# Bias table, its store and the last gate rows earlier in the second FFN of a two-block kernel

## The chip, the cores and the metric

The program runs on one core of one Trainium2 chip. The metric is the device time of that core in microseconds (us), less is better. A core has TensorE (PE, the matrix engine, with PEld for its weight loads), VectorE (DVE), ScalarE (ACT), GpSimd (POOL) and SyncE (SP). SP issues nearly all transfers (DMA) from one queue, in program order, and the core's 16 DMA engines carry them out.

## The reference

Two transformer blocks in sequence work on 256 tokens of width 1024. The first has a SwiGLU feed-forward network (FFN), a mixer of attention and convolution, and a second FFN. The second block has two attentions, an MLP and a gated embedding. All is in float32. The part in which the change lies is the end of the first block:

```python
def swiglu(h, w13, w2):
    gu = jnp.einsum('bsd,df->bsf', h, w13)
    g, u = jnp.split(gu, 2, axis=-1)
    return jnp.einsum('bsf,fd->bsd', jax.nn.silu(g) * u, w2)
...
        mod = (jnp.einsum('bd,dn->bn', c_act, w_ada[l]) + b_ada[l]).reshape(b, N_SUB, 3, D_MODEL)
...
        h = modulate(x, norm_w[l, 2], mod[:, 2, 0], mod[:, 2, 1])
        x = x + 0.5 * mod[:, 2, 2][:, None, :] * swiglu(h, ffn_w13[l, 1], ffn_w2[l, 1])
```

`D_FF` is 2816, that is 22 column blocks of 128. The gate `mod[:, 2, 2]` has 1024 columns, or eight blocks of 128 (numbers 64 to 71 of the 72 in `mod`). The second block of the network needs two tables: cosines and sines of the axial rotary embedding times the norm's gains, and for its dilated attention a bias by relative position (`bias_table[bucket]`, with the band's mask), which is the same for every query but shifted.

## The kernel before

**Weights come in units.** All weights lie in one array in the order of use, cut into units of 128 partitions x 2048 columns (1 MB). Every unit is loaded by SP into one of four raw buffers (`sb_raw`, NR = 4). ACT then writes its rounded half ("hi", `sb_ring`), in two halves of 1024 columns; DVE writes the remainder ("lo", L200), also in two halves. The ring of split units has four places (NS = 4). A matrix product takes three matmuls for each tile: hi x hi, lo x hi, hi x lo. A unit of the FFN's up projection holds the 16 tiles of one column block j, so PE uses one unit for each j, with moving tiles of 258 columns (256 tokens and 2 for the shift).

**A unit of gate rows** (`ada`) is loaded in the same way and in the same four raw buffers, but goes to no matmul: DVE multiplies its two row blocks with silu(c) and sums them (L209, two instructions of 128x1024 and two short reads). The list `ADA_3` says ahead of which unit of the second FFN each of its four gate units stands: position p is ahead of the weights of column block p.

**The order of the work** is written by a planner (`Plan`) as one list of steps; each engine runs those of the list that are its own, in that order. A raw buffer is refilled when its unit has been consumed: the load of unit i on SP waits for the "lo" (or the gate rows) of unit i-4, and SP's later transfers wait behind it. While PE works on block j+1, the planner has ACT and DVE finish block j (`glu_evac2`, below "the finish of block j") and split the weights of block j+3: on ACT the order is hi of j+3, the two shifts of block j (`sb_zb`), silu, `hid_hi`; on DVE two scalings from the banks, first half of lo of j+3, the product, second half of lo, `hid_lo`. The banks form a ring of seven; two are used for each block.

**The tables.** `load_tables` (SP, five small transfers of 960 KB in all, into `R`), `axial_tables` (DVE, seven instructions: one on `sb_bhalf` and six on `R`, which wait for the transfers), `bias_table` (one PE matmul in full float32, 128x512, then one addition on DVE into 12 partitions of `R`) and `bias_store` (SP: the 12 rows of 512 numbers are written to `scratch` in main memory 64 times each, 768 pieces of 2 KB, 1536 KB). `bias_store` waits for the addition. The second block reads the rows back, each with its own shift (`load_bias`), some 200 us later.

In the kernel before, `load_tables` and `axial_tables` stand behind the finish of block 4, `bias_table` and `bias_store` behind that of block 8, and the last gate unit is ahead of block 17.

Of the kernel before, what the change touches and what calls it, by code (L numbers as in the profile page):

```python
# [36 lines left out]
def unit_list():  # L37
# [5 lines left out]
    def chunks(tiles, n=16):  # L43
        return [("w", tiles[i:i + n]) for i in range(0, len(tiles), n)]

    def down(m, n, k0=0):
        return [tile(m, k0 + k, f) for f, ks in down_order(n) for k in ks]
# [4 lines left out]
    def ada_pairs(first, n):  # L52
        return [ada(first + i, first + i + 1) for i in range(0, n, 2)]

    def mix(ws, adas, places):
        out = []
        assert len(adas) == len(places)
        for i, w in enumerate(ws):
            out += [a for a, p in zip(adas, places) if p == i]
            out.append(w)  # L60
        return out

    def ffn_up(m, js):
        return [("w", [t for k in range(8) for t in (tile(m, k, j), tile(m, k, 22 + j))]) for j in js]

    def nat(m, ranges):
        w = sum(b - a for a, b in ranges)
        ks = U // w
        return [("w", [(m, k, a, b) for k in range(k0, k0 + ks) for a, b in ranges]) for k0 in range(0, 8, ks)]
# [22 lines left out]
    ws = ffn_up("w13b", range(22)) + chunks(down("w2b", 22))  # L92
    out += mix(ws, ada_pairs(64, 8), ADA_3)
    ws = nat("win2", [(1024, 1536)]) + nat("win2", [(0, 512)]) + nat("win2", [(512, 1024)])
# [19 lines left out]

ADA_1 = [1, 3, 4, 5, 8, 10, 11, 13, 13, 15, 17, 17, 19, 19, 21, 23]
ADA_2 = [0, 4, 4, 4, 13, 14, 15, 19]
ADA_3 = [5, 6, 9, 17]

PACE, AHEAD, KEEP = 4, 3, 2
TAKE_AFTER = (1, 2, 3)  # L120
# [130 lines left out]
def done(turn, *events):  # L251

    turn.buf.free = events
# [235 lines left out]
class Plan:  # L489
# [546 lines left out]
    def second_ffn(self):  # L1036
        m = self.m
        bk = Ring(m.banks[0:7])
        norm = []

        def begin(k):
            if k == 4:
                norm.append(self.x_norm("f2"))

        def finish(k):
            if k == 2:
                self.norm_rows(norm[0])

        first = self.glu2("f2", bk, 0, begin)
        for j in range(1, NH1):  # L1050
            banks = self.glu2("f2", bk, j, finish if j == 1 else None)
            if j == 1:
                self.glu_evac2("f2", first, 0)
            self.glu_evac2("f2", banks, j)
            if j == 4:
                self.add("load_tables")
                self.add("axial_tables")
            if j == 8:
                b = m.banks[7].take()
                self.add("bias_table", b)  # L1060
                done(b, ("bias_table",))
                self.add("bias_store")
        self.add("gcol", 2, 0.5)
        for f, bank in self.down("f2", bk, NH1, "down"):
            self.residual("f2", f, bank, "m2", True)
# [2419 lines left out]
```

How the kernel before makes its waits and increments, by code:

```python
    def then_inc(self, signal, n):  # L177
        if self.ins is not None:
# [11 lines left out]
    def wait_ge(self, signal, value):  # L190
        if self.passed.get(signal.name, 0) < value:
            self.passed[signal.name] = value
            if self.e is not None:
                self.e.wait_ge(signal.sem, value)
# [287 lines left out]
    def turn(self, *turns):  # L482
        for t in turns:
            for event in t.before:
                self.e.wait_ge(*self.at(*event))
# [930 lines left out]
    def load(self, i):  # L1417
        m, e = self.m, self.e
        if i >= NR:
            kind, blocks = m.units[i - NR]
            if kind == "ada":
                e.wait_ge(*self.at("ada", blocks[-1][1]))
            else:
                e.wait_ge(*self.at("lo", m.windex[i - NR], 1))
        w = m.widths[i]
        src = m.wts[m.offs[i]:m.offs[i] + 128 * w].rearrange("(p w) -> p w", p=128)
        e.dma_start(m.raw[:, i % NR, 0:w], src).then_inc(*self.up(f"unit{i % NR}_in", ("unit", i), by=16))
# [7 lines left out]
    def load_mask(self):  # L1435
        m, e = self.m, self.e
        e.wait_ge(*self.at("x", "f1", 7))
        e.dma_start(m.reg(34, 256), m.cons2_in[:, 0:256]).then_inc(*self.up("mask_in", ("mask",), by=16))
# [1 line left out]
    def load_tables(self):  # L1440
        m, e = self.m, self.e
        e.wait_ge(*self.at("merged_lo", 7))
        e.dma_start(m.reg(45, 256), m.cons2_in[:, OK2["axc"][0]:OK2["axc"][1]]).then_inc(
            *self.up("cosines_in", ("cosines",), by=16))
        e.dma_start(m.reg(44, 256), m.cons2_in[:, OK2["axs"][0]:OK2["axs"][1]]).then_inc(
```

## Time and profile before

| | |
|---|---|
| time, median of 3 runs | 1005.85 us (1005.77 to 1007.15) |
| the profiled execution | 1007.17 us, of which its span is 1005.4 us |
| PE busy | 988.8 us (98%) |
| DVE busy | 771.0 us (77%) |
| ACT busy | 536.6 us (53%) |
| DMA engines, queue of SP | 59.6% of 16 engines, 213 GB/s in the mean |

The times of the rows below are microseconds from the start of the span. A row of the timeline gives start, duration, engine, line, operation, what it writes and reads, and in square brackets how long the engine was idle before it and what ended that. The second FFN's up projection (22 blocks) runs from about 384 to 506 us. Matmul ends are modelled, so a row of PE can seem to overlap the next.

### The profile page before, as it was taken

Reading aid. Unit: us, or ns where it says so; the run is one execution under the profiler, and the core shown is the slowest. Engines: PE = TensorE matmul, PEld = TensorE weight load, DVE = VectorE, ACT = ScalarE, POOL = GpSimd, SP = SyncE. Lnnn points to the kernel's source line nnn. Section 1 sums busy time; section 2 is a strip of 40 time slices with the busy share of each in tenths; the row PEclk is TensorE's granted clock in tenths of the full one; section 3 lists DMA queues with packets and bytes.
Section 4 is the critical chain, followed back from the end, with each engine's and each line's share of the span. In section 5 each row is a group of like instructions: output and inputs, shape, how many; then the busy total and the mean of one; then the engine's idle time right before and its main releaser. Section 6 shows DMA issues by size and latency. Waiting matters only on the chain.

```text
span 1005.4 us, 17440 instructions
## 1 busy us (share of the span) xinstructions
PE 988.8 (98%) x7090; PEld 925.3 (92%) x7090; DVE 771.0 (77%) x1397; ACT 536.6 (53%) x930; POOL 12.0 (1%) x33
## 2 busy tenths in 40 slices
PE   8999999999899999999999999999999999999997
PEld 8999998998898999999988988789999988988896
DVE  6999999879976788685776688547778776677665
ACT  5555554437575565353665446664555554455453
POOL 0000000004000000000000000000000000000000
PEclk9999999999999999999999999999999999999999
DMA  8997998865563555677665435364445555545431
GB/s 334 372 352 260 372 345 327 314 200 211 220 224 130 206 211 184 234 216 230 244 215 201 170 126 209 126 196 126 161 168 181 186 190 187 202 176 177 179 106 42
DMA packets 33678, 213.94 MB, mean 213 GB/s; under 512 B 3773, under 2 KB 6717, under 8 KB 8894
## 3 DMA queue, kind: packets, MB, share of 16 engines
q1 hardware_dynamic: 33310, 211.78, 59.6%
q8 instruction: 56, 0.92, 0.4%
q10 hardware_dynamic: 288, 1.05, 0.3%
q14 instruction: 24, 0.20, 0.1%
HBM read 210.19 MB, written 2.62 MB: 212 GB/s over the span
## 4 chain that ended last, share of the span: by engine, by line
PE 81%; DVE 8%; ACT 4%; DMA 4%; issue 2%; SPq 0%; ACTq 0%; DVEq 0%
PE bank L224 79%; DMA sb_raw<-wts 3%; DVE sb_ring L200 2%; ACT sb_ring L197 2%; PE bank L227 2%; ACT sb_tmp L197 1%; DVE sb_tq L200 1%; DVE sb_junk L209 1%; DVE sb_tmp L200 1%; DMA sb_x<-xt 1%; DMA R<-rows 1%; DVE sb_tmp L206 1%; ACT R L197 0%; DVE R L200 0%; DVE R_512r L200 0%
## 5 line engine op out<-in xcount | busy, mean ns | idle before, releaser
L224 PE MATMUL bank<-sb_h,sb_ring 128*128 128x258 f32 (+2 forms) x3776 | 493.7, 291 | 0.6 <-ACT sb_h L197 0.3
L224 PEld LDWEIGHTS bank<-sb_h,sb_ring 128*128 128x128 f32 x3776 | 472.8, 189 | 14.5 <-issue 2.4
L200 DVE TENSOR_TENSOR sb_ring<-sb_raw,sb_ring 128x1024 fp32r<-128x1024 f32 (+1 forms) x324 | 386.3, 1206 | 10.4 <-ACT sb_ring L197 10.3
L197 ACT ACTIVATE sb_ring<-sb_raw 128x1024 fp32r<-128x1024 f32 (+1 forms) x324 | 320.4, 1037 | 72.0 <-DMA sb_raw<-wts 37.5
L224 PE MATMUL bank<-R_512r,sb_ring 128*128 128x256 f32 (+1 forms) x1608 | 225.7, 301 | 0.0
L224 PEld LDWEIGHTS bank<-R_512r,sb_ring 128*128 128x128 f32 x1608 | 211.5, 188 | 12.0 <-issue 0.5
L224 PE MATMUL bank<-sb_ring,sb_h 128*128 128x512 f32 (+1 forms) x504 | 112.5, 378 | 0.0
L224 PEld LDWEIGHTS bank<-sb_ring,sb_h 128*128 128x128 f32 x504 | 87.4, 188 | 16.6
L209 DVE CUSTOM_DVE_ANT_0 sb_junk<-sb_raw,sb_csil,sb_cols 128x1024 bf16<-128x1024 f32 x72 | 92.3, 1282 | 2.1 <-DMA sb_raw<-wts 0.4
L224 PE MATMUL bank<-R_1024r,sb_ring 128*128 128x512 f32 (+1 forms) x576 | 91.6, 320 | 0.0
L224 PEld LDWEIGHTS bank<-R_1024r,sb_ring 128*128 128x128 f32 x576 | 82.0, 188 | 8.2
L200 DVE TENSOR_TENSOR sb_tq<-bank,sb_rbc 128x256 f32<-128x256 f32 x87 | 33.8, 420 | 52.1 <-ACT sb_zb L197 26.8
L197 ACT ACTIVATE R_512r<-sb_tq 128x256 fp32r<-128x256 f32 x60 | 25.1, 418 | 77.6 <-DVE sb_tq L200 50.6
L197 ACT ACTIVATE sb_tmp<-bank 128x256 f32<-128x256 f32 (+2 forms) x62 | 27.9, 462 | 30.4 <-PE bank L224 27.8
L197 ACT ACTIVATE sb_tmp<-sb_tmp,sb_smx 128x256 f32<-128x256 f32 (+2 forms) x40 | 20.9, 524 | 35.5 <-DVE sb_smx L209 25.3
L206 DVE SCALAR_TENSOR_TENSOR sb_x<-bank,sb_gcol,sb_x 128x256 f32<-128x256 f32 x36 | 17.4, 483 | 27.5 <-PE bank L224 27.0
L197 ACT ACTIVATE sb_h<-sb_x,sb_cols 128x256 fp32r<-128x256 f32 x24 | 14.2, 593 | 37.6 <-DVE sb_x L206 24.0
L200 DVE TENSOR_TENSOR R_512r<-sb_tq,R_512r 128x256 fp32r<-128x256 f32 x60 | 25.2, 420 | 3.9 <-ACT R_512r L197 3.9
L200 DVE TENSOR_TENSOR sb_tmp<-bank,sb_tmp 128x256 f32<-128x256 f32 x32 | 12.4, 425 | 19.1 <-ACT sb_tmp L197 19.0
L197 ACT ACTIVATE sb_tq<-bank 128x256 f32<-128x256 f32 (+1 forms) x35 | 12.9, 367 | 25.7 <-PE bank L224 25.7
L197 ACT ACTIVATE sb_tq<-sb_tq,sb_zb 128x256 f32<-128x256 f32 x26 | 13.3, 510 | 23.6 <-DVE sb_tq L200 23.5
L227 PE MATMUL bank<-sb_con,sb_tmp 128*128 128x128 f32 (+1 forms) x134 | 21.1, 275 | 2.3 <-ACT sb_tmp L197 1.9
(168 smaller groups left out, 576.8 us busy)
## 6 DMA issues: line engine op xcount, KB each, us to landing
sb_raw<-wts SPq DMA_DIRECT2D x193, 1024.0 KB, 4.9
sb_raw<-wts SPq DMA_DIRECT2D x3, 512.0 KB, 3.6
scratch<-R SPq DMA_DIRECT2D x1, 1536.0 KB
sb_x<-xt ACTq DMA_DIRECT2D x2, 512.0 KB, 5.4
R<-scratch SPq DMA_DIRECT2D x2, 508.0 KB, 8.7
sb_raw<-wts SPq DMA_DIRECT2D x1, 768.0 KB, 4.5
sb_raw<-wts SPq DMA_DIRECT2D x1, 640.0 KB, 4.0
R<-scratch SPq DMA_DIRECT2D x2, 258.0 KB, 5.5
```

Source lines behind the costliest of these rows:

```text
L197: return Issued(self.e and self.e.activation(o, i, func, **kw))
L200: return Issued(self.e and self.e.tensor_tensor(*a))
L206: return Issued(self.e and self.e.scalar_tensor_tensor(*a))
L209: return Issued(self.e and self.e.tensor_tensor_reduce(*a))
L224: return Issued(self.e and self.e.matmul(o, w, m, start=start, stop=stop, skip_group_check=True))
L227: return Issued(self.e and self.e.transpose(o, i, ident))
```

## The change

`load_tables` moves from behind the finish of block 4 to behind that of block 1. `axial_tables` stays behind block 4. `bias_table` and `bias_store` move from behind block 8 to behind block 4. The last gate unit (rows 70 and 71) moves from ahead of block 17 to ahead of block 12; the host lays out the array of units in the new order. No instruction is added or removed.

```diff
-ADA_3 = [5, 6, 9, 17]
+ADA_3 = [5, 6, 9, 12]
...
             self.glu_evac2("f2", banks, j)
+            if j == 1:
+                self.add("load_tables")
             if j == 4:
-                self.add("load_tables")
                 self.add("axial_tables")
-            if j == 8:
+            if j == 4:
                 b = m.banks[7].take()
                 self.add("bias_table", b)
                 done(b, ("bias_table",))
                 self.add("bias_store")
```

SP's queue in the second FFN, before. The first row's loads are the last two ahead of the tables (units that become blocks 9 and 10). `R_256_51` to `R_128_55` are the tables' sources, `scratch` is the store's target; a load that waits for `modulation` refills the buffer of a gate unit, one that waits for `weights_lo` the buffer of a weight unit.

```order
L230 DMA sb_raw<-wts 128x2048 [waits weights_lo] x2
L230 DMA R_256_51<-cons 128x256 [waits hidden_lo]
L230 DMA R_256_52<-cons 128x256
L230 DMA R_256_53<-rows 128x256
L230 DMA R_1024_54<-cons 128x1024
L230 DMA R_128_55<-rel 128x128
L230 DMA sb_raw<-wts 128x2048 [waits weights_lo]
L230 DMA sb_raw<-wts 128x2048 [waits modulation]
L230 DMA sb_raw<-wts 128x2048 [waits weights_lo] x3
L230 DMA scratch<-R_512_56 768x1x512 [waits bias_table]
L230 DMA sb_raw<-wts 128x2048 [waits weights_lo] x5
```

The same queue after the change.

```order
L230 DMA R_256_51<-cons 128x256 [waits hidden_lo]
L230 DMA R_256_52<-cons 128x256
L230 DMA R_256_53<-rows 128x256
L230 DMA R_1024_54<-cons 128x1024
L230 DMA R_128_55<-rel 128x128
L230 DMA sb_raw<-wts 128x2048 [waits modulation]
L230 DMA sb_raw<-wts 128x2048 [waits weights_lo]
L230 DMA sb_raw<-wts 128x2048 [waits modulation]
L230 DMA sb_raw<-wts 128x2048 [waits weights_lo] x2
L230 DMA scratch<-R_512_56 768x1x512 [waits bias_table]
L230 DMA sb_raw<-wts 128x2048 [waits weights_lo]
L230 DMA sb_raw<-wts 128x2048 [waits modulation]
```

The tables stand five loads sooner, the store is now where the tables stood, behind the load of block 10. The loads behind the store brought, before, block 16, the gate unit, block 17, block 18; after, they bring block 11, the gate unit, block 12, block 13.

On DVE, after `axial_tables` (first two rows), the addition of the bias table (`R_512_56`) now comes ahead of the finish of block 5 (`sb_tq`).

```order
 L200 TENSOR_TENSOR R_256_139<-R_256_51,R_256_53 128x256
 L200 TENSOR_TENSOR R_256_140<-R_256_52,R_256_53 128x4x32 x2
+L200 TENSOR_TENSOR R_512_56<-bank,R_1024_54 12x512 [waits bias_product,onehot_in]
 L200 TENSOR_TENSOR sb_tq<-bank,sb_rbc 128x256 [waits shift_out,glu]
 L200 TENSOR_TENSOR sb_tq<-bank,sb_rbc 128x256 [waits hidden_lo]
```

On PE the bias product now stands between the matmuls of block 4 and those of block 5.

```order
 L224 MATMUL bank<-sb_h,sb_ring 128x258 [waits weights_lo]
 L224 MATMUL bank<-sb_h,sb_ring 128x258 x23
+L224 MATMUL bank<-R_1024_54,R_128_55 128x512 [waits rel_in,onehot_in,factors_ready]
 L224 MATMUL bank<-sb_h,sb_ring 128x258 [waits weights_lo,up_scaled]
 L224 MATMUL bank<-sb_h,sb_ring 128x258 x2
```

## Rows read from the trace of the kernel before

**Rows 1.** Page, part 1: busy us (share) x instructions.
```profile
PE 988.8 (98%) x7090; PEld 925.3 (92%) x7090; DVE 771.0 (77%) x1397; ACT 536.6 (53%) x930; POOL 12.0 (1%) x33
```
**Rows 2.** Waits, 400 to 480 us: who waited for whom, total us, times, longest.
```profile
DVE R L200 <- DMA R<-rows: 6.7, 1, 6.7
```
**Rows 3.** Timeline of PE and PEld at the only gaps in the up projection.
```profile
471.25 0.90 PEld L224 LDWEIGHTS bank<-sb_h,sb_ring 128*128 128x128 f32 x7 [0.28 <-issue]
477.49 29.00 PE L224 MATMUL bank<-sb_h,sb_ring 128*128 128x258 f32 x240 [0.22 <-DVE sb_ring L200]
```
**Rows 4.** Timeline of ACT: shifts of blocks 2 and 5, between them hi of block 7.
```profile
395.69 0.24 ACT L197 ACTIVATE sb_zb<-bank 128x1 f32<-128x1 f32 x2 [0.50 <-PE bank L224]
...
405.03 1.99 ACT L197 ACTIVATE sb_ring<-sb_raw 128x1024 fp32r<-128x1024 f32 x2
...
412.93 0.23 ACT L197 ACTIVATE sb_zb<-bank 128x1 f32<-128x1 f32 x2 [0.77 <-PE bank L224]
```
**Rows 5.** Timeline of the SP queue, 390 to 444 us: single issues.
```profile
390.99 0.33 SPq L230 DMA_DIRECT2D sb_raw<-wts  x1
396.31 0.33 SPq L230 DMA_DIRECT2D sb_raw<-wts  x1
410.96 0.33 SPq L230 DMA_DIRECT2D sb_raw<-wts  x1
438.93 0.33 SPq L230 DMA_DIRECT2D sb_raw<-wts  x1
439.86 0.95 SPq L230 DMA_DIRECT2D scratch<-R  x1
443.78 0.34 SPq L230 DMA_DIRECT2D sb_raw<-wts  x1
```
**Rows 6.** DMA issues, median of all, then of 443.78 and 453.48: us to landing.
```profile
sb_raw<-wts SPq DMA_DIRECT2D x193, 1024.0 KB, 4.9
...
sb_raw<-wts SPq DMA_DIRECT2D x1, 1024.0 KB, 23.2
...
sb_raw<-wts SPq DMA_DIRECT2D x1, 1024.0 KB, 18.4
```
**Rows 7.** Windows of 1 us around the store; last columns PEclk, DMA share, GB/s.
```profile
444.00:445.00 1.00, 1.00 (x11) 1.00 (x10) 0.09 (x1) 1.00 (x4) 0.00 (x0) 1.00 0.72 96
...
462.00:463.00 1.00, 1.00 (x11) 1.00 (x10) 0.00 (x0) 0.00 (x0) 0.00 (x0) 1.00 1.03 358
```
**Rows 8.** Timeline of DVE: the tables' instructions.
```profile
411.19 0.17 DVE L203 TENSOR_SCALAR sb_bhalf<-sb_cols 128x16 f32<-128x16 f32 x1
418.10 1.57 DVE L200 TENSOR_TENSOR R<-R,R 128x256 f32<-128x256 f32 x6 [6.75 <-DMA R<-rows]
...
439.16 0.67 DVE L200 TENSOR_TENSOR R<-bank,R 12x512 f32<-12x512 f32 x1
```
**Rows 9.** Timeline of DVE behind the landing at 467.03 us, and its second wait.
```profile
469.25 0.76 DVE L200 TENSOR_TENSOR sb_tq<-bank,sb_rbc 128x256 f32<-128x256 f32 x2 [10.61 <-ACT sb_zb L197]
469.93 1.21 DVE L200 TENSOR_TENSOR sb_ring<-sb_raw,sb_ring 128x1024 fp32r<-128x1024 f32 x1
...
476.12 1.22 DVE L200 TENSOR_TENSOR sb_ring<-sb_raw,sb_ring 128x1024 fp32r<-128x1024 f32 x1
```
**Rows 10.** Timeline of ACT: hi of blocks 16 and 17, then the shifts of block 21.
```profile
467.03 2.01 ACT L197 ACTIVATE sb_ring<-sb_raw 128x1024 fp32r<-128x1024 f32 x2 [9.41 <-DMA sb_raw<-wts]
...
471.95 2.01 ACT L197 ACTIVATE sb_ring<-sb_raw 128x1024 fp32r<-128x1024 f32 x2
...
509.10 0.21 ACT L197 ACTIVATE sb_zb<-bank 128x1 f32<-128x1 f32 x2
```
**Rows 11.** PE's two longer waits elsewhere, and the window behind the second.
```profile
232.10 1.17 PE L224 MATMUL bank<-sb_ring,R_512r 128*128 128x512 f32 x5 [1.11 <-ACT sb_tq L197]
...
272.79 0.64 PE L227 MATMUL bank<-sb_con,R 128*96 128x128 f32 x4 [2.97 <-ACT R L197]
...
274.00:276.00 2.00, 2.00 (x13) 1.97 (x12) 2.00 (x4) 1.09 (x4) 0.00 (x0) 0.56 0.87 328
```

## The prediction

> **What bounds the kernel now.** I read the page's busy times first: PE is busy 988.8 of 1005.4 us [rows 1], so the most that any edit off PE can give back is what PE waits. Then the waits and the timelines between 380 and 510 us, the up projection that the change touches, to see who waits and whether it reaches PE. DVE waits 6.7 us for the tables [rows 2] and ACT 9.41 us for a weight unit [rows 10]; the reader is to see that these are not PE's. PE itself has two gaps there: 0.28 us of its weight load ahead of block 16 and 0.22 us ahead of block 17 [rows 3]. So the second FFN can give back 0.5 us and no more. The question of this case is whether the new places keep PE as well covered as the old ones.
>
> **PE's clock of blocks.** ACT's shifts of a block start the moment PE has finished it, where ACT was waiting for PE: block 2 at 395.69 and block 5 at 412.93 [rows 4], thus (412.93 - 395.69) / 3 = 5.75 us for a block. From there 11 blocks end at 412.93 + 63.25 = 476.18. PE stood ready for block 17 at 477.49 - 0.22 = 477.27 [rows 3]. The 1.09 us between are the 0.28 us gap and the bias product, which is so 0.81 us. Without any wait block 17 would have begun at 476.18 + 0.81 = 476.99; it began at 477.49, and the two gaps together cost 0.50 us.
>
> **Why PE waits there: the store.** SP issues the load that ends ahead of the store at 438.93, the store at 439.86 and the load of block 16 at 443.78 [rows 5]. An ordinary unit lands 4.9 us after its issue, that of block 16 takes 23.2 us [rows 6] and lands at 467.0. Between them the engines are busy but move little (96 GB/s at a share of 0.72), until 358 GB/s are back at 462 [rows 7]: the 1.5 MB of the store, in pieces of 2 KB out of 12 partitions, take some 20 us, and what is queued behind waits. Two loads later the landing is at 453.48 + 18.4 = 471.88, so behind the store units land every (471.88 - 466.98) / 2 = 2.45 us. ACT begins hi of block 16 at 467.03 and of block 17 at 471.95 [rows 10]. DVE gets to the finish of block 13 at 469.25, to lo of block 16 at 469.93 and, after the gate rows, to lo of block 17 at 476.12 [rows 9]. Call L the landing of the first weight unit behind the store. Then PE can begin that unit's block at about L + 4.2 (end of the first half's lo, 469.93 + 1.21, and a little), and the next block at L + 10.46 (477.49 - 467.03). The gate unit between the two costs DVE about 2.5 us of that.
>
> **Part 1, tables behind block 1.** Five DMAs now follow the load issued at 390.99 [rows 5]. DVE's six table instructions had to wait from 411.36 to 418.10 [rows 8]. So tables issued from 391.4 should be in by 391.4 + 6.8 = 398.2, long before DVE wants them (411.4) and before PE wants the product (407.2). Removed: 6.75 us of DVE, but nobody on PE waited for them, since no gap stands between 412 and 471 us [rows 3]: gain 0. Queued behind them on SP is the load of block 7, issued at 396.31 [rows 5], which ACT wants at 405.03 [rows 4]. Ordinary landing is 401.2; if it moves only when the tables are through, 398.2 + 4.9 = 403.1. Cost 0, with 1.9 us of cover left.
>
> **Part 2, bias product and addition behind block 4.** Moved, not added: 0.81 us of PE and 0.67 us of DVE [rows 8] in either place. On DVE the finish of block 4 ends at 411.19; 0.17 + 1.57 + 0.67 us of table work [rows 8] bring it to 413.6. PE ends block 5 at 412.93 + 0.81 = 413.74, so DVE is there in time: cost 0. DVE and ACT now have no backlog. In the kernel before they carried one from 418 us to the end of the phase: the shifts of block 21 run at 509.10 [rows 10], while PE ends that block at about 477.49 + 28.8 = 506.3. It has no price on PE, as no gap follows it; its end gives nothing.
>
> **Part 3, the store behind block 4.** It is issued at 413.6, 26.2 us sooner than the 439.86 of before. The load ahead of it is that of block 10 at 410.96 [rows 5]; the load of block 11 follows when lo of block 8 is through: DVE starts the finish of block 5 at about 414.1 and needs about 3.4 us to there (0.7 for the scalings, two halves of 1.2 and the product between them, by the pattern of rows 9), so at 417.5. When does block 11 land? From one side: as long behind the landing of the load ahead of the store as before. That was 438.93 + 4.9 = 443.8 to 467.0, 23.2 us; now 410.96 + 4.9 + 23.2 = 439.1. From the other side: as long behind the store's issue as before, 467.0 - 439.86 = 27.1 us; now 440.7. I take 439.5, near the first: the store of before stood behind a load that still moved, now it is issued only 2.3 us ahead of that load's landing, and a transfer has about 4.9 - 2.45 = 2.45 us before its data move, so it starts at 416.0 and not at 415.6 or so.
>
> **Part 4, who needs it.** Before, the first unit behind the store was that of block 16. PE was due there at 476.99 - 5.75 = 471.24, 4.2 us after the landing: just covered. Now it is the unit of block 11, since one of the four raw buffers holds the gate rows ahead of block 9 when the store is issued. PE is due at block 11 at 412.93 + 5 x 5.75 + 0.81 = 442.49, and at block 12 at 448.24. The last gate unit moved with the store and stands again between the two, so the sequence on ACT and DVE is that of rows 9 and 10. Block 11 can begin at 439.5 + 4.2 = 443.7 (wait 1.2 us) and block 12 at 439.5 + 10.46 = 449.96, which is 1.72 us later than without waits. From then on ACT and DVE need about 4.9 us for a block (hi to hi, 467.03 to 471.95 [rows 10]) and PE 5.75, so nothing more is lost. At block 17 the old 0.50 us are gone. **Sum: +1.72 - 0.50 = +1.2 us.** With the two ends of the landing it is +0.8 (439.1) and +2.4 (440.7).
>
> **A rule against the rows.** The store's 2 KB pieces run at about 1.57 MB / 20 us = 79 GB/s [rows 6, 7]. The Trainium skill, "DMA: Bandwidth & Descriptors", section Specifications, puts the smallest transfer for line rate at 512 B, which these pieces exceed fourfold. By that rule the store would be through in some 4 us at the rate around it, no load would be late in either kernel, and the sum would be 0. The trace disagrees, with 23.2 us for a unit behind the store.
>
> **The rivals.**
> *A. Forecast*, PE waits about 1.7 us at blocks 11 and 12, a net +1.2 us. For: the same four loads follow the store in the same order, and every interval is taken from rows.
> *B. The store drains sooner*, because it has another time or other traffic beside it. PE would wait nowhere from L = 437.8 on: the sum is the 0.5 us removed, -0.5 us. Against: 1.7 us less of 23.2 without a reason.
> *C. Slower.* The store's drain counts from its own issue, L = 440.7, and PE's first wait becomes 2.4 us. The granted clock was 0.56 in the window behind a wait of 2.97 us, and stayed whole behind one of 1.11 us [rows 11]. Mine of 1.2 us lies near the harmless one, that of 2.4 us nearer the other. Price: +2.4 us without the clock. In the window at the lower clock 13 matmuls ran in 2 us [rows 11], against 17 at 5.75 us for a block's 48, so each such window costs 4 x 0.12 = 0.5 us; two or three of them add 1.0 to 1.5 us, up to +3.9 us in all. It decides from L = 440.3 on (sum over 2 us).
> *D. The change does not do what it says:* the tables come sooner, but DVE's wait was never paid by PE, and a gain of 2 us or more has no wait to come from; only a gap that this trace does not show would give it.
>
> **How the numbers follow.** The measurement of this kernel can tell about 0.2%, or 2 us, from no change. Chances: A 0.68, B 0.10, C 0.18, and 0.04 for a gain over 2 us by D's unseen gap. A and B lie within 0.2%; a little of A's spread passes 2 us. So faster 0.04, same 0.76, slower 0.20. The profiled execution was 1007.17 us around a span of 1005.4; the sum gives it a span of 1006.6 and 1008.4 us. The median of the runs was 1005.85, and 1.2 us on it make 1007.0. Range: down to B (1005.3), up to C without the whole price of the clock (1008.9).
>
> **What would show it.** In the profile after: DVE's wait for the tables is gone, DVE adds the bias table near 413 us and the store is issued at 413.6; a load issued near 417.5 takes 21 to 23 us; ACT idles about 11 us up to 439.5; PE waits about 1.2 us near 443 and 0.5 us near 449 for DVE's `sb_ring`; none at 477. I am wrong if PE shows no wait in 440 to 450 us (B), if the first wait exceeds 2 us or the granted clock falls there (C), if ACT waits for block 7 near 405 us (part 1), or if a stage far from here has another time.

## The result, and the profile after

| | before | after |
|---|---|---|
| time, median of 21 runs each | 1005.82 us (1004.46 to 1008.30) | 1007.32 us (1006.30 to 1008.89) |
| ratio after / before | | 1.0014, 95% interval 1.0008 to 1.0021 |
| profiled execution, its span | 1007.17 us, 1005.4 us | 1007.19 us, 1005.4 us |
| PE busy in it | 988.8 us | 988.0 us |

The change costs 1.4 us (0.8 to 2.1), which is inside the 0.2% that the prediction calls the same. Yet the two profiled executions are equally long. Two rows tell why. SP's issue of the load ahead of the tables' old and new neighbourhood stood at 390.99 us [rows 5]; after the change it stands at 389.53:

```profile
389.53 0.33 SPq L230 DMA_DIRECT2D sb_raw<-wts  x1
...
411.98 0.95 SPq L230 DMA_DIRECT2D scratch<-R  x1
```

So 1.46 us were already won before the first moved instruction ran. Windows of 2 us at the start (us, busy and count of PE, PEld, DVE, ACT, POOL, then PEclk, DMA share, GB/s), first of before, then of after, show where:

```profile
12.00:14.00 2.00, 2.00 (x12) 2.00 (x11) 1.79 (x7) 1.06 (x1) 0.00 (x0) 0.50 0.99 418
```
```profile
12.00:14.00 2.00, 1.73 (x16) 1.53 (x15) 1.82 (x6) 1.34 (x2) 0.00 (x0) 1.00 1.01 426
```

In the profiled execution of before the granted clock was 0.50 here (1.2 GHz), behind a wait of PE of 1.0 us that ended at 9.6 us; in that of after this wait was 0.5 us and the clock stayed 1.00 (2.4 GHz). The length of that wait doesn't decide it: in e10 (below) it was 0.20 us, and the clock fell all the same:

```profile
10.00:12.00 2.00, 2.00 (x10) 2.00 (x11) 1.79 (x9) 0.39 (x1) 0.00 (x0) 0.50 1.00 422
```

The program is the same up to there, and the executions of both kernels scatter by some 3 us. A pair of spans can therefore not be compared at this size; a stretch between two marks can. I take from SP's issue above to the first matmul of the down projection:

```profile
506.31 8.94 PE L224 MATMUL bank<-R_512r,sb_ring 128*128 128x512 f32 x50
```

After: 506.31 - 389.53 = 116.78 us. Before: 506.33 - 390.99 = 115.34 us. The stretch is longer by **1.44 us**, and what follows it is the same to 0.1 us (1005.4 less 506.3 in both).

Counted by the first matmul of each block in the trace, a block without a wait takes 5.75 us. After the change PE needed 7.47 us from the start of block 10 to that of block 11, then 6.20 and 5.85 us, which is 2.27 us too much. Before, it needed 6.01 us from block 15 to 16, then 6.20 and 5.85 us, which is 0.81 us too much. The difference is 1.46 us.

The waits of 400 to 480 us after (engine, tile, line, waited for: total, times, longest), to be read beside [rows 2]:

```profile
ACT sb_ring L197 <- DMA sb_raw<-wts: 11.4, 1, 11.4
...
PE bank L224 <- DVE sb_ring L200: 1.8, 2, 1.6
```

DVE's 6.7 us for the tables are gone; ACT's wait for a unit has grown from 9.4 to 11.4 us, and PE's own from 0.2 to 1.8. The timelines of DVE, ACT, PE and PEld after, to be read beside [rows 3, 8, 10]:

```profile
409.80 1.56 DVE L200 TENSOR_TENSOR R<-R,R 128x256 f32<-128x256 f32 x6
411.28 0.67 DVE L200 TENSOR_TENSOR R<-bank,R 12x512 f32<-12x512 f32 x1
```
```profile
438.28 2.01 ACT L197 ACTIVATE sb_ring<-sb_raw 128x1024 fp32r<-128x1024 f32 x2 [11.43 <-DMA sb_raw<-wts]
```
```profile
442.54 6.01 PE L224 MATMUL bank<-sb_h,sb_ring 128*128 128x258 f32 x48 [1.56 <-DVE sb_ring L200]
448.74 31.52 PE L224 MATMUL bank<-sb_h,sb_ring 128*128 128x258 f32 x261 [0.19 <-DVE sb_ring L200]
```
```profile
442.51 5.83 PEld L224 LDWEIGHTS bank<-sb_h,sb_ring 128*128 128x128 f32 x48 [1.74 <-issue]
448.71 31.45 PEld L224 LDWEIGHTS bank<-sb_h,sb_ring 128*128 128x128 f32 x262 [0.37 <-issue]
```

The issue at 416.13 us of the unit of block 11, to its landing (KB, us), and a window of 2 us in which the store had the engines to itself:

```profile
sb_raw<-wts SPq DMA_DIRECT2D x1, 1024.0 KB, 22.1
```
```profile
414.00:416.00 2.00, 2.00 (x19) 2.00 (x18) 2.00 (x3) 0.99 (x2) 0.00 (x0) 1.00 0.70 82
```

The two waits of PE stand ahead of blocks 11 and 12, 48 matmuls (one block) apart; the one at 477 us is gone.

### The profile page after: what moved, and what is told of

Read it like the earlier page. It is cut to its first block, busy times and chain, and to the rows that moved or that the text cites. A ratio compares the mean times of both kernels' runs of the same rounds, so it can differ in the third digit from the quotient of the medians.

```text
span 1005.4 us, 17440 instructions
## 1 busy us (share of the span) xinstructions
PE 988.0 (98%) x7090; PEld 924.6 (92%) x7090; DVE 771.0 (77%) x1397; ACT 537.2 (53%) x930; POOL 12.0 (1%) x33
## 3 DMA queue, kind: packets, MB, share of 16 engines
q10 hardware_dynamic: 288, 1.05, 0.3%
## 4 chain that ended last, share of the span: by engine, by line
PE 84%; DVE 7%; DMA 3%; ACT 3%; issue 2%; SPq 0%; ACTq 0%; DVEq 0%
PE bank L224 83%; DMA sb_raw<-wts 3%; DVE sb_ring L200 2%; PE bank L227 2%; ACT sb_ring L197 2%; ACT sb_tmp L197 1%; DVE sb_junk L209 1%; DVE sb_tmp L200 1%; DVE sb_tmp L206 1%; DVE sb_tq L200 1%; ACT R L197 0%; DVE sb_tmp L203 0%; DVE R_512r L200 0%; DVE sb_st_v L212 0%; DVE sb_tmp L209 0%
## 5 line engine op out<-in xcount | busy, mean ns | idle before, releaser
L200 DVE TENSOR_TENSOR sb_ring<-sb_raw,sb_ring 128x1024 fp32r<-128x1024 f32 (+1 forms) x324 | 386.2, 1205 | 11.4 <-ACT sb_ring L197 11.3
L197 ACT ACTIVATE sb_tmp<-bank 128x256 f32<-128x256 f32 (+2 forms) x62 | 27.9, 461 | 30.5 <-PE bank L224 27.8
L197 ACT ACTIVATE sb_tmp<-sb_tmp,sb_smx 128x256 f32<-128x256 f32 (+2 forms) x40 | 20.9, 524 | 35.5 <-DVE sb_smx L209 25.3
L200 DVE TENSOR_TENSOR R_512r<-sb_tq,R_512r 128x256 fp32r<-128x256 f32 x60 | 25.2, 419 | 3.9 <-ACT R_512r L197 3.9
L197 ACT ACTIVATE sb_tq<-bank 128x256 f32<-128x256 f32 (+1 forms) x35 | 12.8, 366 | 25.8 <-PE bank L224 25.8
L197 ACT ACTIVATE sb_zb<-bank 128x1 f32<-128x1 f32 x76 | 9.6, 160 | 24.4 <-DVE sb_tq L200 12.9
```

The costliest lines, as they stand in the source:

```text
L197: return Issued(self.e and self.e.activation(o, i, func, **kw))
L200: return Issued(self.e and self.e.tensor_tensor(*a))
```

## The experiments

The theory: PE pays the landing of the first weight unit behind the store, one us for one us, once it comes later than PE is due at its block less 4.2 us. What counts is which block that unit is (the cover) and how long the store holds the loads behind it (the drain). The first half can be read in every trace: in all seven profiles in which PE waits for that unit (before, after, e1, e2, e5, e7, e8), its block starts 4.26 or 4.27 us behind ACT's first use of it, whether that use is at 436.7 or at 467.0 us. Rivals: the place of the gate rows by itself, the tables' loads, or the queue in which the store stands.

The mark-to-mark stretch of every profiled execution, from the same two rows of each, and the time against the kernel before on the same chip:

| kernel | stretch, us | above 114.5 | store's issue to ACT's use of the next unit | ratio to before (95%) |
|---|---|---|---|---|
| before | 115.34 | 0.84 | 27.2 | 1 |
| changed | 116.78 | 2.28 | 26.3 | 1.0014 (1.0008 to 1.0021) |
| changed, again (e7) | 115.73 | 1.23 | 25.3 | 1.0015 (1.0005 to 1.0025) |
| gate unit back at 17 (e1) | 115.21 | 0.71 | 25.2 | 1.0017 (1.0009 to 1.0026) |
| gate unit alone (e2) | 122.26 | 7.76 | 26.3 | 1.0082 (1.0070 to 1.0095) |
| tables alone (e3) | 114.51 | 0.01 | 25.8 | 1.0002 (0.9993 to 1.0012) |
| store issued by ACT (e5) | 115.93 | 1.43 | 25.5 | 1.0028 (1.0018 to 1.0038) |
| extra pieces (e8) | 119.29 | 4.79 | 27.8 | 1.0044 (1.0031 to 1.0057) |
| store in halves (e4, twice) | 114.50, 114.51 | 0.0 | 16.8 (first half) | 0.9986 (0.9977 to 0.9994), 1.0001 (0.9992 to 1.0009) |
| 96 rows (e9, twice) | 114.50, 114.51 | 0.0 | no wait | 1.0005 (0.9996 to 1.0015), 0.9998 (0.9989 to 1.0006) |
| 96 rows, old places (e10) | 114.50 | 0.0 | no wait | 1.0004 (0.9995 to 1.0013) |

114.50 or 114.51 us is what the stretch takes without a wait, in six profiles. Each stretch is that of one execution, the ratio that of all. The fourth column differs by 2 us between kernels with the same store, and the store's 2 KB pieces in the traces tell why. They move for 19.5 to 20.8 us in every kernel that stores them at once from 12 partitions. The first piece comes 3.1 to 3.2 us behind the store's issue where the store stands behind block 8 (before, e2, e3), and 1.6 to 1.7 us where it stands behind block 4; it comes 4.14 us behind the issue of the load ahead in before and 4.15 us after. From the last piece to ACT's use of the unit it is another 3.0 to 4.1 us, and this part scatters: 4.1 in the changed kernel, 3.1 in the same program again (e7).

**One part undone: the gate unit back ahead of block 17 (e1).**

```diff
-ADA_3 = [5, 6, 9, 12]
+ADA_3 = [5, 6, 9, 17]
```

> The changed kernel with one part undone: the last gate unit is ahead of block 17 again; tables behind block 1, bias product and store behind block 4 as changed. Theory (PE pays for the cover in front of the store: the first weight unit behind the store is block 11 and lands about 23 us after the landing of the load ahead of it): the load behind the store still brings block 11, so PE waits about 1.7 us ahead of block 11 as in the changed kernel; the 0.2 us ahead of block 12 goes, since no gate rows stand on DVE between the two splits. About 0.2 to 0.4 us less than changed, thus +1.0 us against before. Rival (the gate rows' new place is what costs): the time falls back to that of before and no wait of PE stands in 435 to 450 us.

ACT's and PE's rows:

```profile
436.71 2.01 ACT L197 ACTIVATE sb_ring<-sb_raw 128x1024 fp32r<-128x1024 f32 x2 [10.30 <-DMA sb_raw<-wts]
```
```profile
440.97 63.48 PE L224 MATMUL bank<-sb_h,sb_ring 128*128 128x258 f32 x528 [0.43 <-DVE sb_ring L200]
```

The wait ahead of block 11 stays, the one ahead of block 12 is gone, as expected. The first is shorter than expected (0.43 us, not 1.7), because the unit landed 1.1 us sooner behind the store than in the changed kernel. The profile alone would not refute the rival, for its stretch (115.21) is no longer than that of before, and it is the fastest of the 11 executions (1005.17 us). The median is 1006.66 us, 1.7 above before on the same chip, and its interval is clear of no change. So the rival falls by the median and by the wait that stays: the gate rows' new place is not what costs in the changed kernel.

**The other part alone: the gate unit ahead of block 12, the store behind block 8 (e2).**

```diff
-ADA_3 = [5, 6, 9, 17]
+ADA_3 = [5, 6, 9, 12]
```

> The kernel before with only the last gate unit moved, from ahead of block 17 to ahead of block 12; tables behind block 4 and store behind block 8 stay. Theory: one of the four raw buffers now holds the gate rows when the store is issued at about 439.9 us, so the first weight unit behind the store is block 15 instead of block 16, landing at 467 us again. PE is due there 5.75 us sooner, at 465.5, and can start at 467.0 + 4.2 = 471.2: a wait of about 5.7 us, less the 0.5 us of before, thus +5.2 us against before (about 1011.0); if the granted clock falls behind so long a wait, 1 to 1.5 us more. Rival (the gate unit's place is of no account, only when the store is issued): the time of before within 0.5 us.

ACT, PE, and two windows of 2 us behind PE's wait:

```profile
467.03 2.00 ACT L197 ACTIVATE sb_ring<-sb_raw 128x1024 fp32r<-128x1024 f32 x2 [11.40 <-DMA sb_raw<-wts]
```
```profile
471.29 35.88 PE L224 MATMUL bank<-sb_h,sb_ring 128*128 128x258 f32 x276 [4.93 <-DVE sb_ring L200]
```
```profile
470.00:472.00 2.00, 0.71 (x3) 0.74 (x4) 2.00 (x4) 0.71 (x3) 0.00 (x0) 0.57 0.67 283
472.00:474.00 2.00, 2.00 (x11) 2.00 (x10) 1.01 (x2) 2.00 (x4) 0.00 (x0) 0.50 0.54 180
```

The store is issued as long behind the first mark as before (440.78 - 391.92 = 48.86 us, before 48.87), and ACT uses the unit behind it 0.9 us sooner after the issue (26.3 against 27.2 us; that both stand at 467.03 is chance, since this execution runs 0.93 us later from its start). But PE now waits 4.93 us for it, since the unit is that of block 15. This is the strongest of the experiments for the cover: one number of a table is worth 8.2 us of the time (1.0082), and 6.9 us of the stretch. Of the stretch, 5.1 us are the wait (10.84 us from block 14 to 15 instead of 5.75) and 2.7 us the clock in the block behind it (8.41 us), less the 0.8 us of before. At 0.50 a window of 2 us counts 11 matmuls, at the whole clock 19 (478 to 480 us):

```profile
478.00:480.00 2.00, 2.00 (x19) 2.00 (x18) 1.05 (x3) 1.35 (x4) 0.00 (x0) 1.00 0.79 176
```

The expectation (5.2, with the clock up to 6.7) was low, since the clock was down from about 470 to 477 us, in four such windows, where I had allowed for two or three, and since each costs more than I had counted (17 matmuls against 13, where the same view counts 19 at the whole clock). The wait follows from one block of cover: the 0.26 us lost there before, plus 5.75, less the 0.9 us by which the unit came sooner, make 5.1.

**The tables' loads alone (e3).**

```diff
+            if j == 1:
+                self.add("load_tables")
             if j == 4:
-                self.add("load_tables")
                 self.add("axial_tables")
```

> The kernel before with only the tables' loads moved, from behind block 4 to behind block 1; bias product and store behind block 8, last gate unit ahead of block 17. Theory: DVE's wait of 6.7 us for the tables is gone, ACT and DVE carry no backlog, so the addition of the bias table runs about 4 us sooner (435 to 436 us instead of 439.2) and the store with it. The unit behind it, block 16, lands about 4 us sooner (463), PE is due there at 471.2 and has cover: no wait of PE for the ring in 400 to 510 us, and the 0.5 us of before are gone: -0.5 us against before, -1.9 us against the changed kernel. Rival (tables in front of block 7's load cost as much as they give): no gain, or a wait of ACT for a DMA near 404 us.

SP and ACT:

```profile
433.00 0.95 SPq L230 DMA_DIRECT2D scratch<-R  x1
```
```profile
458.79 2.01 ACT L197 ACTIVATE sb_ring<-sb_raw 128x1024 fp32r<-128x1024 f32 x2 [3.56 <-DMA sb_raw<-wts]
```

No wait of PE is left and the stretch is at its floor. The store is issued 5 us sooner relative to the first mark (433.00 - 389.18 = 43.8 against 439.86 - 390.99 = 48.9) for the same block 16, as expected. The tables' loads cost nothing at their new place. The stretch is 0.83 us shorter than before, so DVE's wait for the tables did reach PE in the kernel before, by way of the store: it held up the addition of the bias table, the store was issued 5 us later for the same block, and the unit behind it missed PE's block. In the time, the expected gain of 0.5 us is inside the interval (0.9993 to 1.0012) and not shown.

**The store in ScalarE's queue (e5).** The function `bias_store` moves from SyncE's to ScalarE's steps, in the changed order.

```diff
-                 "bias_store": self.bias_store, "load_bias": self.load_bias, "load_p": self.load_p,
+                 "load_bias": self.load_bias, "load_p": self.load_p,
...
-        steps = {"exp_ready": self.exp_ready, "hi": self.hi, "load_x": self.load_x,
+        steps = {"exp_ready": self.exp_ready, "hi": self.hi, "bias_store": self.bias_store, "load_x": self.load_x,
```

> The changed kernel with the store of the bias table issued by ScalarE instead of SyncE, at the same place in the order, so that it stands in another queue than the weight loads. Theory (units are late because they stand behind the store's pieces in SP's queue): the engines now alternate between the two queues, a unit issued during the store lands in some 8 to 12 us instead of 22, ACT hardly waits for a DMA in 427 to 440 us, PE waits nowhere there: -1.9 us against the changed kernel, -0.5 us against before. Rival (the 16 engines are held by the slow pieces whichever queue they come from): units still land after 20 us and more, and the time is that of the changed kernel.

ACT's timeline, then the issue at 420.25 us of the next unit (KB, us to landing):

```profile
413.15 1.38 ACTq L230 DMA_DIRECT2D scratch<-R  x1
...
438.60 2.01 ACT L197 ACTIVATE sb_ring<-sb_raw 128x1024 fp32r<-128x1024 f32 x2 [8.01 <-DMA sb_raw<-wts]
```
```profile
sb_raw<-wts SPq DMA_DIRECT2D x1, 1024.0 KB, 18.3
```

My theory of the queue fell here, the rival holds: the unit stands in another queue and still lands only 25.5 us behind the store. The store's pieces take 20.5 us from this queue too: the engines themselves are held. And ACT now waits for DVE's addition and issues for 1.4 us. The kernel is slower than before (1.0028); whether it is slower than the changed one is not shown, since the intervals overlap (1.0018 to 1.0038, against 1.0008 to 1.0021 and 1.0005 to 1.0025) and the two were not run on one chip.

**The changed kernel again (e7), as the reference of its group.** Its edit is one blank line.

> The changed kernel as it is (one blank line added), as the reference for the other kernels of this group on the same chip. Theory: the second FFN's up projection takes 1.4 us more than before, by PE's waits ahead of blocks 11 and 12; the median is 1.0 to 2.0 us above the kernel before.

```profile
438.52 2.01 ACT L198 ACTIVATE sb_ring<-sb_raw 128x1024 fp32r<-128x1024 f32 x2 [10.39 <-DMA sb_raw<-wts]
```
```profile
442.79 5.99 PE L225 MATMUL bank<-sb_h,sb_ring 128*128 128x258 f32 x48 [0.53 <-DVE sb_ring L201]
448.99 57.71 PE L225 MATMUL bank<-sb_h,sb_ring 128*128 128x258 f32 x480 [0.21 <-DVE sb_ring L201]
```

The same two waits, and a dose by accident: from the store's issue to ACT's use of the unit it is 25.3 us (438.52 - 413.24) instead of 26.3, and the stretch is shorter by 1.05 us. So in this execution it is 0.39 us longer than that of before, where 1.4 was expected. The median, 1007.37 against 1005.73 us, is again 1.5 us above before by the ratio (1.0015).

**The store in two halves (e4).**

```diff
-                self.add("bias_store")
+                self.add("bias_store", 0, 32)
+            if j == 12:
+                self.add("bias_store", 32, 32)
...
-    def bias_store(self):
+    def bias_store(self, a=0, n=64):
...
-        dst = m.scratch[:, :].rearrange("h (m w) -> h m w", m=64)[:, :, 0:512]
+        dst = m.scratch[:, :].rearrange("h (m w) -> h m w", m=64)[:, a:a + n, 0:512]
...
-        e.dma_start(dst, m.reg(51, 512)[0:12, :].unsqueeze(1).to_broadcast([12, 64, 512])).then_inc(
+        e.dma_start(dst, m.reg(51, 512)[0:12, :].unsqueeze(1).to_broadcast([12, n, 512])).then_inc(
```

> The changed kernel with the store in two halves of 32 copies, one at its place behind block 4 and one behind block 12. Theory (PE pays for the length of the drain beyond the cover of the ring): each half drains in some 10 us, the unit behind the first lands near 428 us instead of 438.3, that behind the second about 13 us after its issue; both are inside the cover, PE waits nowhere between 400 and 510 us. -1.9 us against the changed kernel, -0.5 us against before. Rival (that a store stands there costs, not its length): a wait of PE remains at block 11, or comes again at blocks 19 and 20.

ACT, PEld, and the issues of the unit behind each half:

```profile
428.58 2.01 ACT L197 ACTIVATE sb_ring<-sb_raw 128x1024 fp32r<-128x1024 f32 x2 [1.92 <-DMA sb_raw<-wts]
```
```profile
406.12 97.67 PEld L224 LDWEIGHTS bank<-sb_h,sb_ring 128*128 128x128 f32 x815 [0.24 <-issue]
```
```profile
sb_raw<-wts SPq DMA_DIRECT2D x1, 1024.0 KB, 12.6
...
sb_raw<-wts SPq DMA_DIRECT2D x1, 1024.0 KB, 11.1
```

The units behind the halves land in 12.6 and 11.1 us instead of 22, and the weight loads run for 97 us without a gap: PE waits for neither half. The same bytes cost nothing when no single transfer outlasts the cover. The second half also stands behind block 12 instead of block 4, so it is the pair of shorter drains, each with a cover of its own, that was tried, not the cut alone. In this group the halves are faster than the changed kernel (1004.66 us against 1007.37, and 0.9977 to 0.9994 against 1.0005 to 1.0025).

**The same store read from 96 partitions (e9).** The host repeats each head's column of the relative bias and each row of the band eight times, so that the product and the addition make eight copies of each row.

```diff
-        dst = m.scratch[:, :].rearrange("h (m w) -> h m w", m=64)[:, :, 0:512]
+        dst = m.scratch[:, :].rearrange("h (r m w) -> (h r) m w", r=8, m=8)[:, :, 0:512]
...
-        e.dma_start(dst, m.reg(51, 512)[0:12, :].unsqueeze(1).to_broadcast([12, 64, 512])).then_inc(
+        e.dma_start(dst, m.reg(51, 512)[0:96, :].unsqueeze(1).to_broadcast([96, 8, 512])).then_inc(
...
-        e.tensor_tensor(m.reg(51, 512)[0:12, :], b.ap[0:12, :], m.reg(46, 1024)[0:12, 512:1024], ALU.add).then_inc(
+        e.tensor_tensor(m.reg(51, 512)[0:96, :], b.ap[0:96, :], m.reg(46, 1024)[0:96, 512:1024], ALU.add).then_inc(
...
-    rel[0:32, 0:12] = v["rel_bias_2"]
+    rel[0:32, 0:96] = np.repeat(v["rel_bias_2"], 8, axis=1)
...
-        band[h] = [
+        band[8 * h:8 * h + 8] = [
```

> The changed kernel, but the bias table is made on 96 partitions (each head's row eight times; the host repeats the columns of the two inputs), so that the same 768 pieces of 2 KB are read from 96 partitions instead of 12. It tells what the 20 us of the store hang on. If on the reading of 12 partitions: the drain is much shorter (5 to 10 us), the unit of block 11 lands before 430 us, PE waits nowhere, -1.9 us against the changed kernel. If on the pieces themselves or on writing them to memory: units land as late as before, and the time is that of the changed kernel. The theory of cover holds in both cases and asks only that PE's wait follow the landing: wait = landing + 4.2 us less the time at which PE is due at block 11.

Windows of 2 us while it drains (store issued at 411.76), and the unit issued at 415.91:

```profile
414.00:416.00 2.00, 2.00 (x19) 2.00 (x18) 2.00 (x4) 1.22 (x2) 0.00 (x0) 1.00 1.01 325
416.00:418.00 2.00, 2.00 (x19) 2.00 (x19) 1.97 (x4) 1.29 (x4) 0.00 (x0) 1.00 1.05 355
```
```profile
sb_raw<-wts SPq DMA_DIRECT2D x1, 1024.0 KB, 8.7
```

The rates of a window are those of all transfers in it. The store's own 2 KB pieces, counted in the trace, made 325 and 314 GB/s in these two windows, where those from 12 partitions made 77 GB/s over their 20.5 us (1.57 MB) after and 78 over their 20.2 us before. The 768 pieces are through in 5.9 us instead of 20.5, one of them takes 0.08 us instead of 0.29 (median), and the unit lands in 8.7 us instead of 22. So the drain hangs on the partitions that are read, not on the 768 pieces nor on writing them to memory. A single piece is 3.5 times as fast, so it is not only that more of the 16 engines may have had pieces to move, which was not told apart. ACT waits for no transfer and PE for no unit. In the time, this group alone doesn't tell the kernel from the changed one by their intervals against before (1.0005, 0.9996 to 1.0015); the second group, below, does (0.9998, at most 1.0006, where the changed kernel has at least 1.0008 in the result).

**More behind the store (e8).**

```diff
+        e.dma_start(m.scratch[:, :].rearrange("h (m w) -> h m w", m=64)[:, 0:16, 512:764],
+                    m.reg(51, 512)[0:12, 0:252].unsqueeze(1).to_broadcast([12, 16, 252])).then_inc(
+            *self.up("extra_out", ("extra",), by=16))
```

> The changed kernel with a second small store right behind the first: 192 pieces of 1 KB into columns of the scratch array that nothing reads. Theory: this goes one to one into PE's wait, since the cover is already used up. At the store's piece rate (768 in 20 us) it is 5 us, at its byte rate 2.5 us, so block 11's unit lands 2.5 to 5 us later and the time is 2.5 to 5 us above the changed kernel, 1 to 1.5 us more if the granted clock falls. Rival (PE's wait in the changed kernel is not set by the landing): the time moves by less than 1 us.

ACT, PE, and a window of 2 us behind the wait:

```profile
440.91 2.00 ACT L197 ACTIVATE sb_ring<-sb_raw 128x1024 fp32r<-128x1024 f32 x2 [12.92 <-DMA sb_raw<-wts]
```
```profile
445.17 62.08 PE L224 MATMUL bank<-sb_h,sb_ring 128*128 128x258 f32 x504 [3.05 <-DVE sb_ring L200]
```
```profile
448.00:450.00 2.00, 2.00 (x12) 2.00 (x11) 1.96 (x6) 1.36 (x5) 0.00 (x0) 0.50 0.80 332
```

Against e7 of the same group the unit lands 2.5 us later behind the store (27.8 against 25.3). That fits the forecast by the byte rate (2.5 us) and not that by the piece rate (5 us), which the scatter of 1 us between executions can't bridge. PE's first wait grows by 2.5 us (3.05 against 0.53): one for one. The granted clock falls to 0.50 behind this wait of 3.05 us. The median is 1010.62 against 1007.37 us, +3.3.

**Is one of them faster than before?** The halves had 0.9986 in their group, more than the theory allows, and the 96 rows 1.0005 with the same profile. So both ran again, and the 96 rows also in the old places.

> The store in two halves (behind blocks 4 and 12), once more, since its median was 1.1 us below before where no wait of PE in the profile of before is worth more than 0.5 us. Theory (only PE's wait behind the store is saved): its lowest times are those of the kernel before, 1004.5 us, and its median is 0.3 to 1.0 us below before. If the gain is more than that in both groups, before must lose more behind its store in most executions than in the profiled one.

> The store read from 96 partitions in the changed order, once more: its profile showed no wait of PE in the up projection (114.5 us for it, as little as the halves), but its median was 1.7 us above the halves'. Theory (the two are equal, the medians of 12 executions scatter by what happens at the start): median within 0.7 us of the halves of this group and below the kernel before. Rival (something outside the second FFN is slower with it): again 1 us and more above the halves.

> The store read from 96 partitions, but issued behind block 8 and with the last gate unit ahead of block 17 as in the kernel before; the tables' loads behind block 1. Theory (with a short drain the place is of no account): the unit behind the store lands in less than 10 us, no wait of PE for the ring between 400 and 510 us, and the time is that of the 96-partition store behind block 4, within 0.7 us.

For the old places, the issue of the unit behind the store, to its landing:

```profile
sb_raw<-wts SPq DMA_DIRECT2D x1, 1024.0 KB, 8.0
```

Now the order is reversed: the halves at 1.0001 (0.9992 to 1.0009), the 96 rows at 0.9998 (0.9989 to 1.0006), in the old places 1.0004 (0.9995 to 1.0013). The medians are 1005.54, 1004.72 and 1005.98 us, so two expectations of "within 0.7 us" were missed (0.8 us between the halves and the 96 rows, 1.3 us between the two places of the 96 rows), while the stretches of all three are 114.50 or 114.51 us. As far as the profiles show, what makes medians of 11 executions differ by over 1 us lies outside the stretch. All of them and before share their lowest times (1004.4 to 1004.6 us), the changed kernel's are 1006.30 and 1005.65. So before seems to lose nothing behind its store in its best executions, while the best of the changed kernel's 32 is 1.2 us above these. The gain of the halves over before was not repeated. In the old places (e10) the tables' loads are early too, and e3 has no wait there with the store of 12 rows. So e10 shows no cost of that place, but not that the short drain is what removes it. Both versions are better than the changed kernel and free of the waits; that either beats the kernel before by the 0.8 us of its stretch is not shown.

## Why the prediction was right

It said +1.2 us, between 0.8 and 2.4 by the two ends of the landing; measured are 1.4 (0.8 to 2.1), in the stretch of the profiles 1.44. The mechanism is the forecast one. That this pair of profiles agrees so closely is in part luck: the same program again (e7) has a stretch only 0.39 us longer than before's, while the medians of the two sets of runs are 1.4 and 1.5 us above before by their ratios.

- **Part 1 and part 2: right for the sum, wrong in one reason.** The tables' loads cost nothing, and the bias product costs PE the same in either place (0.88 us by the starts of the blocks, forecast 0.81). But DVE's wait for the tables and the backlog were not without a price in the kernel before: they put the store 5 us later, and e3, which removes them alone, takes away the whole 0.83 us of PE's loss. In the change this is no second gain, since the store moves anyway and the sum takes that loss off in part 4. It also means that the second FFN could give back 0.8 us and not 0.5.
- **Part 3: right.** Corrected by the 1.46 us of the earlier start, the store is issued at 413.44 (forecast 413.6) and the unit used at 439.74 (439.5). The store does start with the landing of the load ahead of it, as the first end (439.1) has it: its first piece comes 4.15 us behind that load's issue, before 4.14. The 0.64 us beyond this end are 0.3 us of longer drain and 0.35 us between the last piece and ACT's use, and the latter is the part that scatters by 1 us between executions. So 439.5 was near for this execution, by no stronger reason.
- **Part 4: right, with both terms too small by nearly as much.** PE lost 2.27 us at the blocks behind the store where 1.72 was forecast, and in the kernel before 0.81 where 0.50 was read. Block 12 began 10.46 us behind ACT's use of the unit of block 11, as forecast, and block 11 itself 4.26 us behind it (forecast 4.2). What was off is when PE is due: the clock of blocks began at ACT's shift at 412.93, and PE's first matmul of block 6 is at 412.67. With the small errors of the other steps, PE was due 0.21 us sooner than the sum has it, in both kernels. Another 0.10 us, in both, are lost in the block behind the second wait. These errors cancel in the difference, which is luck; what is left of it, 0.24 us, is the later landing of part 3. e1, e2 and e8 confirm the structure: which block the unit behind the store belongs to, and the one-for-one price.
- **The rule at odds with the rows** did not hold, as the trace said: pieces of 2 KB exceed 512 B and still took 20 us. e9 gives the missing condition. The Trainium skill names it elsewhere, in "SBUF — State Buffer", section "Door 1: The DMA port swizzle": the rate of a transfer goes by how many of 16 ports its partitions reach, four partitions beside one another to a port at about 27 GB/s each. By that the 12 partitions reach three ports, an estimate of 82 GB/s and 19 us for the 1.57 MB; the trace agrees (the pieces ran at 77 GB/s for 20.5 us), and e9's 96 partitions, which by the section's table of ports reach all 16, ran at 314 to 325 GB/s.
- **Rivals.** B (a sooner drain) is what e4 and e9 made on purpose. C (slower) did not come for the changed kernel in its profiles, where PE's single waits stayed at 1.6 us and the clock whole; its mechanism is real, as e2 and e8 show, and its price per us of landing was right. The price that it gives the clock, 1.0 to 1.5 us, fits e8 (about 1.0 us, by the block behind the wait against the same block of the changed kernel) and is too low for e2 (2.7 us).
- **Span.** I forecast a span of 1006.6 for the profiled execution. It was 1005.4, because the profiled execution of before had the lower clock at its start and this one had not, and so reached the first mark 1.46 us sooner. The sum should have been made against a stretch, not a span.

## What to carry to other kernels

A transfer in a shared queue is free only as long as it drains within the cover of the loads behind it; to move it, find the first load behind it and the moment at which the slowest engine is due there, for each engine that holds a buffer may have shifted that load by a whole block. Before looking for a better place, make it shorter or cut it: with halves, or a source on more partitions, no wait was left in any profile, and of the placements only the tables' loads alone (e3) did as well. A wait of another engine that seems to be paid by nobody can still set when a transfer starts: DVE's did. And compare differences of a us between two fixed marks of the traces, of several executions, not between spans.

## What the runs showed of the hardware

- A store from SBUF that reads 12 partitions ran at 77 GB/s, from 96 partitions at 314 to 325 GB/s (e9), with the same 2 KB pieces.
- While the narrow store drained, a 1 MB load in the queue of another engine was held as well (18.3 us to landing, e5), though the loads were not behind it in a queue. Why the engines don't alternate was not tried.
- The granted clock fell to 0.50 behind PE waits of 3.05 us (e8) and 4.93 us (e2, for about 7 us), and stayed whole behind 1.56 us. The length of the wait alone doesn't settle it: a wait of 2.9 to 3.0 us near 272 us is in all thirteen profiles; the clock fell behind it in ten of them and stayed whole in e2 (2.97 us), e7 (2.96 us) and the second profile of the halves (2.98 us). The window behind the wait in e7, then in after (wait 2.95 us):

```profile
272.00:274.00 2.00, 1.47 (x13) 1.48 (x14) 2.00 (x4) 1.05 (x2) 0.00 (x0) 1.00 0.98 410
```
```profile
272.00:274.00 2.00, 2.00 (x12) 2.00 (x11) 2.00 (x5) 0.64 (x3) 0.00 (x0) 0.50 0.91 340
```

- The start of the program sometimes has a stretch at the lower clock and sometimes not. In the profiles with it the first mark stands at 390.7 to 391.0 us (before, e5, e8, e10), and at 391.9 in e2, where it lasted longer; in most without it at 389.1 to 389.5. It is not the only thing that moves an execution: e7 and the second profile of the halves had none and reached the mark at 390.80 and 389.94.
